# Turning the attention weights of two query tiles in one step of a hybrid attention and convolution encoder layer on Trainium2

## The chip, the cores and the metric

The kernel runs on one core of a Trainium2 chip. The metric is the device time of one execution in microseconds (us), as a median of several runs. The core has five engines that run their own instruction streams and meet at semaphores: PE (TensorE, matrix products and transposes), DVE (VectorE), ACT (ScalarE), POOL (GpSimd) and SP (SyncE, which here only starts transfers).

## What is computed

One encoder layer is applied to a prompt of 2048 frames and to 64 further frames of a running stream, model width 1024. In parallel to a convolution module the layer has an attention of 8 heads of width 64, whose weights come from products of sigmoids and not from a softmax:

```python
def _sb_block(qb, qpos, k, v, kpos):
    z = jnp.einsum('bqhd,bkhd->bhqk', qb, k) * scale
    mask = kpos[None, :] < qpos[:, None]
    log_1m_beta = jnp.where(mask, jax.nn.log_sigmoid(-z), 0.0)
    between = lax.cumsum(log_1m_beta, axis=3, reverse=True) - log_1m_beta
    a = jnp.where(mask, jnp.exp(jax.nn.log_sigmoid(z) + between), 0.0)
    return jnp.einsum('bhqk,bkhd->bqhd', a, v)

def _layer(x, ...):
    proj = _rmsnorm(x, g_mix) @ w_in          # 1024 -> 1024 (conv) + 3 x 512 (q, k, v)
    ...                                        # c: gated causal convolution, LayerNorm, swish, 512x512
    o = _stick_breaking(q, k_all, v_all, q_pos, k_pos)
    x = x + jnp.concatenate([c, o], axis=-1) @ w_out
    f = jax.nn.relu(_rmsnorm(x, g_ff) @ w_ff1) # 1024 -> 4096
    x = x + (f * f) @ w_ff2                    # 4096 -> 1024
```

So a[t, s] = beta[t, s] times the product of (1 - beta[t, j]) over s < j < t, strictly causal, and the output is a @ v.

## The kernel before

**Chunks and windows.** The prompt is worked on in four chunks of 512 frames, 0 to 3. The attention of chunk c + 1 is not a phase of its own: it is spread over the feed-forward of chunk c. `window(c)` walks over 128 slots, 16 for each of 8 parts `e` of the hidden units (18 a part in the last window). A slot is 12 matmuls of 512 columns on PE; slots 0 to 7 of a part are the first product (two slots make one group of hidden units, which ACT takes through relu, square and the high half `hid_hi`, and DVE through the low half `hid_lo`), slots 8 to 15 the second product, whose results DVE adds to `resid`. `att_steps(n, slot)` says which steps of the attention are written behind a slot's own work: two steps a slot for chunk 3 (slots 39 to 115), a little more than one for chunk 2, about one for chunk 1. The attention of chunk 0 and that of the 64 running frames are in the same code.

**Pieces and steps.** A piece is the scores of one head and one query tile of 128 rows (`t` is 0 or 1, the two tiles of a pair) against one block of up to 512 keys. Pieces are numbered through by `z`: chunk 1 has 32 to 95, chunk 2 has 96 to 191, chunk 3 has 192 to 319. The two tiles of a pair follow each other, the even number first. For each head and pair the blocks are walked from the diagonal one (`diag`) back to the first, since the product of (1 - beta) is carried on. Below, step 215 is the step in which the scores of piece 215 are computed. `att_piece(c, step, delay)` gives the piece whose turn it is `delay` steps later. The work on piece z is:

- step z: PE the scores (`scores`, L2498, 2 matmuls) into one of two PSUM banks; DVE the mask of a diagonal piece (L2035); ACT two sigmoids, `stay` = 1 - beta (L1581) and `beta` (L1582), each into one of four buffers.
- step z + 1: DVE the running product over `stay` from the right (the scan, L2047; ahead of it a copy of one column, L2046, for a block that is not diagonal); POOL `beta` times `stay` (L1277).
- step z + 3 (`TURN`): PE turns the weights, one transpose for each 128 keys (`turn`, L2508), into one of two PSUM banks (`T_BANK`, by z % 2); ACT rounds the turned weights to the high half of `aT` (the cast, L1593).
- step z + 4: DVE computes the low half of `aT` as the difference (the low, L2057), which frees the bank.
- step z + 5 (`VALUES`), for the odd tile only: PE multiplies both tiles of the pair by the values (`values`, L2529 in chunks 1 to 3).

When a pair's last block is done, ACT and DVE take the output out of PSUM into `osb` (L2076, L2080) and split it into `ohl` (L2069).

**What waits for what.** The order of instructions on each engine is the order of the code. `turn` waits for POOL's product and for the low of the piece two before, which had the same PSUM bank:

```python
            def turn(q):
                pe.wait_ge(s_a, q.z + 1)
                if q.z >= 2:
                    pe.wait_ge(t_lo, q.z - 1)
```

ACT's sigmoids of piece z wait for `t_ps`, the transposes of piece z - 4, since they write its `beta` buffer. `values` waits for `t_lo` of its odd piece and, at a pair's first block, for `o_sum` (the output of the pair before is out of PSUM). In a slot of the window PE writes the 12 matmuls and then all steps. ACT writes relu and square, the sigmoids of the slot's first step, `hid_hi`, the casts of the first step, and then the second step. DVE writes the scan and low of the first step, the additions to `resid`, the mask, `hid_lo`, and then the scan and low of the second step.

Of the kernel before, what the change touches and what calls it, by code (L numbers as in the profile page):

```python
# [55 lines left out]
TURN, VALUES, TAIL = 3, 5, 9  # L56
# [28 lines left out]
ATT = attention()  # L85


def passes(c):
    return [ATT[c, kind] for kind in range(2 if c == NC - 1 else 1)]
# [6 lines left out]
def att_piece(c, step, delay):  # L96

    for seq in passes(c):
        if step < len(seq) + TAIL:
            k = step - delay  # L100
            return seq[k] if 0 <= k < len(seq) else None
        step -= len(seq) + TAIL
    return None


def att_end(c, what):
# [223 lines left out]
def build(nc, x_prompt, x_sample, cache_k, cache_v, state_conv, g_mix, w_in, w_dw, b_dw, g_cn, b_cn, w_pw,  # L330
# [3 lines left out]
    with ctx:  # L334
# [321 lines left out]
        def stay_of(z):  # L656
            return stay[z % 3] if z < OPENING else stay[z % 4]
# [83 lines left out]
        def out_store(o):  # L741

            return o_st[o % 2], 16 * (o // 2 + 1 + (o == att_end(NC - 1, "o") - 1))
# [5 lines left out]
        def side_by_side(q):  # L749

            return q.o >= att_end(0, "o") and not q.kind

        def summed(o):

            return o + max(0, min(o, att_end(NC - 1, "o") - 1) - att_end(0, "o"))
# [598 lines left out]
        def _(act):  # L1354
# [134 lines left out]
            def front():  # L1489
                evs = kvq_events(1)  # L1490
                for t in range(FRONT):
# [25 lines left out]
                    for step in steps[:1]:  # L1517
                        att_later(0, step)
# [63 lines left out]
                nc.scalar.activation(beta[q.z % 4][0:q.r, 0:q.n], z, ACT.Sigmoid).then_inc(s_sg, 1)  # L1582

            def att_later(c, step):
                q = att_piece(c, step, TURN)
                if q:
                    act.wait_ge(t_ps, q.z + 1)
                    if q.t == 0 and q.v >= 2:
                        act.wait_ge(v_ps, q.v - 1)
                    bank = ps[:, T_BANK + q.z % 2, :]  # L1590
                    full = q.n // P
                    if full:
                        ins = nc.scalar.copy(aT[:, q.v % 2, 0:full, 0, q.t * P:q.t * P + q.r],  # L1593
                                             bank[:, 0:full * q.r].rearrange("p (a b) -> p a b", a=full))
                    if q.n % P:
                        w = q.n % P
                        ins = nc.scalar.copy(aT[0:w, q.v % 2, full, 0, 0:q.r], bank[0:w, full * q.r:(full + 1) * q.r])
                    ins.then_inc(t_hi, 1)
                q = att_piece(c, step, VALUES + 1)
                if q and q.out:  # L1600
                    act.wait_ge(o_sum, summed(q.o + 1))
                    if q.o >= 2:
                        act.wait_ge(*out_store(q.o - 2))
                    me = slice(0, P) if q.kind else slice(q.head % 2 * HD, q.head % 2 * HD + HD)
                    nc.scalar.copy(ohl[q.o % 2][me, 0, :], osb[me, :]).then_inc(o_hi, 1)
                q = att_piece(c, step, VALUES)
                if q and q.out:
                    act.wait_ge(v_ps, q.v + 1)
                    if q.o:
                        act.wait_ge(o_lo, q.o)  # L1610
                    for me, there, here in halves(q):
                        ins = nc.scalar.copy(here(osb[me:me + HD, :]), there(ps[HD - me:P - me, O_BANK, :]))
                    ins.then_inc(o_cp, 1)
# [178 lines left out]
        def _(dve):  # L1792
# [244 lines left out]
            def att_parts(c, step):  # L2037
                q = att_piece(c, step, 1)
                if q:
                    v = stay_of(q.z)  # L2040
                    dve.wait_ge(s_stay, q.z + 1)
                    init = 1.0
                    if not q.diag:
                        dve.wait_ge(s_scan, q.z - 1)
                        init = stay_of(q.z - 2)[0:q.r, 0:1]
                        nc.vector.tensor_copy(v[0:q.r, q.n:q.n + 1], init).then_inc(s_edge, 1)  # L2046
                    nc.vector.tensor_tensor_scan(v[0:q.r, 0:q.n][:, ::-1], v[0:q.r, 0:q.n][:, ::-1],  # L2047
                                                 ones[0:q.r, 0:1].to_broadcast([q.r, q.n]), init,
                                                 ALU.mult, ALU.mult).then_inc(s_scan, 1)
                q = att_piece(c, step, TURN + 1)  # L2050
                if q:
                    dve.wait_ge(t_hi, q.z + 1)
                    bank = ps[:, T_BANK + q.z % 2, :]
                    full = q.n // P
                    o = q.v % 2
                    if full:
                        ins = nc.vector.tensor_tensor(aT[:, o, 0:full, 1, q.t * P:q.t * P + q.r],  # L2057
                                                      bank[:, 0:full * q.r].rearrange("p (a b) -> p a b", a=full),
                                                      aT[:, o, 0:full, 0, q.t * P:q.t * P + q.r].bitcast(F32), ALU.subtract)
                    if q.n % P:  # L2060
                        w = q.n % P
                        ins = nc.vector.tensor_tensor(aT[0:w, o, full, 1, 0:q.r], bank[0:w, full * q.r:(full + 1) * q.r],
                                                      aT[0:w, o, full, 0, 0:q.r].bitcast(F32), ALU.subtract)
                    ins.then_inc(t_lo, 1)
                q = att_piece(c, step, VALUES + 2)
                if q and q.out:
                    me = slice(0, P) if q.kind else slice(q.head % 2 * HD, q.head % 2 * HD + HD)
                    dve.wait_ge(o_hi, q.o + 1)
                    nc.vector.tensor_tensor(ohl[q.o % 2][me, 1, :], osb[me, :], ohl[q.o % 2][me, 0, :].bitcast(F32),  # L2069
                                            ALU.subtract).then_inc(o_lo, 1)  # L2070
                q = att_piece(c, step, VALUES + 1)
                if q and q.out:
                    dve.wait_ge(o_cp, q.o + 1)
                    for me, there, here in halves(q):
                        home = here(osb[me:me + HD, :])
                        ins = nc.vector.tensor_tensor(home, there(ps[me:me + HD, O_BANK, :]), home, ALU.add)  # L2076
                    ins.then_inc(o_sum, 1)
                    if side_by_side(q):
                        dve.wait_ge(o_sum, summed(q.o) + 1)
                        nc.vector.tensor_tensor(home, ps[me:me + HD, O_BANK, 2 * P:4 * P], home, ALU.add).then_inc(o_sum, 1)  # L2080
# [214 lines left out]
        def _(pe):  # L2295
# [244 lines left out]
            def att(c, step):  # L2540
                if q := att_piece(c, step, 0):
                    scores(c, q)
                if q := att_piece(c, step, TURN):
                    turn(q)
                if q := att_piece(c, step, VALUES):
                    values(c, q)
# [229 lines left out]
```

## Time and profile before

| | us |
|---|---|
| median of 3 runs | 2756.15 (2755.06 to 2759.61) |
| the profiled execution, its own time | 2761.99 |
| its span in the trace | 2760.2 |
| PE busy | 2663.6 (96%) |
| DVE busy | 1797.6 (65%) |
| ACT busy | 1121.9 (41%) |
| POOL busy | 592.7 (21%) |

Busy time is the union of an engine's instructions; the span is the time from the first to the last of them. The profiled execution took 5.84 us more than the median and 1.8 us more than its span. Times of day below are us from the start of the span. A row of the timeline gives start, duration, engine, line, operation, operands and how many instructions were merged, and in brackets the idle time of the engine before it and what ended it. The duration of a matmul contains its latency, so what it costs PE is read from one start to the next.

### The profile page before, as it was taken

What the parts mean: (1) busy time and instruction counts of PE and PEld (TensorE: products, weight loads), DVE (VectorE), ACT (ScalarE), POOL (GpSimd) and SP (SyncE); (2) the same over time, 40 slices, a digit from 0 to 9 for tenths busy, and PEclk for the clock granted to TensorE, in tenths of its full rate; (3) what the DMA queues carried; (4) which work ended last, traced back from release to release, by engine and by line L of the source; (5) the groups of instructions that cost most, each with busy time, mean ns of one, the idle gap of its engine ahead of it and who ended that gap; (6) DMA issues with size and microseconds to landing.
All of it is one profiled execution on the core that took longest, in us unless ns stands there. A gap on an engine that the chain in (4) does not pass through costs nothing. (4 is left out here: it accounts for less than half of the span.)

```text
span 2760.2 us, 36720 instructions
## 1 busy us (share of the span) xinstructions
PE 2663.6 (96%) x13304; PEld 2223.3 (81%) x13304; DVE 1797.6 (65%) x2824; ACT 1121.9 (41%) x2221; POOL 592.7 (21%) x523
## 2 busy tenths in 40 slices
PE   8988899999999999999999999999999999999999
PEld 6757778788887887788888797778777877889998
DVE  6996777577773576377775358736888851755444
ACT  4434524455552122355554112334666630333342
POOL 2222210022220010032221002103333310533230
PEclk9999999999999999999999999999999999999999
DMA  9795797697669568455554746854455447355452
GB/s 330 254 351 191 233 354 279 252 332 267 254 219 371 225 228 280 177 218 186 178 181 157 305 183 224 269 197 155 145 191 175 162 161 293 123 189 177 168 198 96
DMA packets 294750, 616.14 MB, mean 223 GB/s; under 512 B 23665, under 2 KB 188529, under 8 KB 250029
## 3 DMA queue, kind: packets, MB, share of 16 engines
q1 hardware_dynamic: 294573, 613.80, 62.8%
q8 instruction: 109, 1.79, 0.3%
q14 instruction: 68, 0.56, 0.1%
HBM read 444.79 MB, written 168.94 MB: 222 GB/s over the span
## 5 line engine op out<-in xcount | busy, mean ns | idle before, releaser
L1277 POOL TENSOR_TENSOR beta<-beta,stay 128x512 f32<-128x512 f32 (+3 forms) x328 | 319.1, 974 | 882.2 <-DVE stay L2047 850.9
L2297 PE MATMUL ps<-h2T_hi,w_s 128*128 128x512 f32 (+2 forms) x976 | 369.6, 379 | 7.6 <-DMA w_s<-w_scratch 3.5
L2299 PE MATMUL ps<-h2T_hi,w_s 128*128 128x512 f32 (+2 forms) x976 | 359.2, 368 | 0.0
L2298 PE MATMUL ps<-h2T_lo,w_s 128*128 128x512 f32 (+2 forms) x976 | 358.7, 367 | 0.0
L1581 ACT ACTIVATE stay<-ps 128x512 f32<-128x512 f32 (+3 forms) x328 | 174.7, 533 | 343.7 <-PE ps L2498 213.3
L2570 PE MATMUL ps<-w_s,hid_hi 128*128 128x512 f32 x768 | 307.2, 400 | 0.0
L2572 PE MATMUL ps<-w_s,hid_hi 128*128 128x512 f32 x768 | 300.1, 391 | 0.0
L2571 PE MATMUL ps<-w_s,hid_lo 128*128 128x512 f32 x768 | 299.6, 390 | 0.0
L2204 DVE TENSOR_TENSOR resid<-ps,resid 128x512 f32<-128x512 f32 x256 | 173.8, 685 | 182.4 <-PE ps L2572 181.9
L2047 DVE TENSOR_TENSOR_SCAN stay<-stay,stay,ones 128x512 f32<-128x512 f32 x192 | 268.7, 1400 | 0.0
L1839 DVE SCALAR_TENSOR_TENSOR cacc<-uT,vecs,cacc 128x512 f32<-128x512 f32 (+1 forms) x360 | 259.7, 777 | 1.5
L2214 DVE TENSOR_TENSOR hid_lo<-ps,hid_hi 128x512 fp32r<-128x512 f32 x96 | 66.2, 690 | 257.3 <-ACT hid_hi L1722 257.3
L2297 PEld LDWEIGHTS ps<-h2T_hi,w_s 128*128 128x128 f32 x976 | 185.1, 190 | 38.7 <-DMA w_s<-w_scratch 3.7
L2299 PEld LDWEIGHTS ps<-h2T_hi,w_s 128*128 128x128 f32 x976 | 184.7, 189 | 30.8
L2298 PEld LDWEIGHTS ps<-h2T_lo,w_s 128*128 128x128 f32 x976 | 185.3, 190 | 27.0 <-issue 1.0
L2057 DVE TENSOR_TENSOR aT<-ps,aT 128x512 fp32r<-128x512 f32 (+3 forms) x328 | 189.5, 578 | 14.1 <-ACT aT L1593 8.2
L2498 PE MATMUL ps<-a_k,a_q 128*128 128x512 f32 (+3 forms) x640 | 185.6, 369 | 9.0 <-DMA a_k<-k_scratch 8.4
L2508 PE MATMUL ps<-ident,beta 128*128 128x128 f32 (+1 forms) x1104 | 175.0, 273 | 10.3 <-DVE aT L2057 10.0
L1593 ACT CAST aT<-ps 128x512 fp32r<-128x512 f32 (+3 forms) x328 | 174.2, 531 | 19.1 <-PE ps L2508 14.6
L1582 ACT ACTIVATE beta<-ps 128x512 f32<-128x512 f32 (+3 forms) x328 | 173.9, 530 | 0.0
L2508 PEld LDWEIGHTS ps<-ident,beta 128*128 128x128 f32 (+1 forms) x1104 | 133.9, 140 | 44.7 <-issue 17.9
L2572 PEld LDWEIGHTS ps<-w_s,hid_hi 128*128 128x128 f32 x768 | 144.2, 188 | 31.8
(268 smaller groups left out, 5640.6 us busy)
## 6 DMA issues: line engine op xcount, KB each, us to landing
w_s<-w_scratch SPq DMA_DIRECT2D x254, 1024.0 KB, 8.0
w_scratch<-w_s SPq DMA_DIRECT2D x94, 1024.0 KB, 8.6
w_raw<-in_w_ff SPq DMA_DIRECT2D x92, 512.0 KB, 5.4
a_k<-k_scratch SPq DMA_DIRECT2D x80, 256.0 KB, 3.7
a_v<-v_scratch SPq DMA_DIRECT2D x80, 256.0 KB, 4.0
a_q<-q_scratch SPq DMA_DIRECT2D x64, 256.0 KB, 4.2
w_s<-w_scratch SPq DMA_DIRECT2D x28, 512.0 KB, 6.5
w_raw<-in_w_in SPq DMA_DIRECT2D x20, 512.0 KB, 8.1
```

The source lines that it names most:

```text
L1277: nc.gpsimd.tensor_tensor(v[0:q.r, 0:n], v[0:q.r, 0:n], stay_of(q.z)[0:q.r, 1:n + 1], ALU.mult).then_inc(s_a, 1)
L1839: nc.vector.scalar_tensor_tensor(out=acc, in0=uT[:, k, tap:tap + wd], scalar=vecs[:, k, tap:tap + 1], in1=acc, op0=ALU.mult, op1=ALU.add). ...
L2047: nc.vector.tensor_tensor_scan(v[0:q.r, 0:q.n][:, ::-1], v[0:q.r, 0:q.n][:, ::-1], ones[0:q.r, 0:1].to_broadcast([q.r, q.n]), init, ALU.mu ...
L2057: ins = nc.vector.tensor_tensor(aT[:, o, 0:full, 1, q.t * P:q.t * P + q.r], bank[:, 0:full * q.r].rearrange("p (a b) -> p a b", a=full), a ...
L2297: nc.tensor.matmul(out, w[0], x[0], start=start, stop=False)
L2298: nc.tensor.matmul(out, w[0], x[1], start=False, stop=False)
L2299: return nc.tensor.matmul(out, w[1], x[0], start=False, stop=stop)
L2498: ins = nc.tensor.matmul(ps[0:q.r, Z_BANK + q.z % 2, 0:q.n], x, a_k[:, k0:k0 + q.n], start=v == 0, stop=v == 1)
L2508: ins = nc.tensor.transpose(ps[0:w, T_BANK + q.z % 2, b * q.r:(b + 1) * q.r], beta[q.z % 4][0:q.r, b * P:b * P + w], ident[0:q.r, 0:q.r])
L2570: nc.tensor.matmul(o, hid_hi[x][:, k, q0:q0 + r], wh[:, c0:c0 + BANK], start=k == 0, stop=False)
L2571: nc.tensor.matmul(o, hid_lo[x][:, k, q0:q0 + r], wh[:, c0:c0 + BANK], start=False, stop=False)
L2572: ins = nc.tensor.matmul(o, hid_hi[x][:, k, q0:q0 + r], wl[:, c0:c0 + BANK], start=False, stop=k == 3)
```

## The change

In chunks 1 to 3, for the prompt's pieces, nothing is turned for the even tile at its own step: its transposes, its cast and its low are written one step later, directly before those of the odd tile. One PE step so has eight transposes in a row (fewer at a diagonal block), four into each of the two banks, and the next step has none; likewise for the two casts on ACT and the two lows on DVE. Steps of scores, sigmoids, scans, products of POOL and `values` stay where they are, and so do chunk 0 and the running frames. No instruction is added or removed and no wait condition is changed.

```diff
@@ -101,6 +101,14 @@
             return seq[k] if 0 <= k < len(seq) else None
         step -= len(seq) + TAIL
     return None
+
+
+def turned_pieces(c, step, delay):
+
+    q = att_piece(c, step, delay)
+    if q is None or (c and not q.kind and q.t == 0):
+        return []
+    return [ATT[c, 0][q.z - ATT[c, 0][0].z - 1], q] if c and not q.kind else [q]
@@ -1582,8 +1590,7 @@
             def att_later(c, step):
-                q = att_piece(c, step, TURN)
-                if q:
+                for q in turned_pieces(c, step, TURN):
                     act.wait_ge(t_ps, q.z + 1)
@@ -2047,8 +2054,7 @@
-                q = att_piece(c, step, TURN + 1)
-                if q:
+                for q in turned_pieces(c, step, TURN + 1):
                     dve.wait_ge(t_hi, q.z + 1)
@@ -2540,7 +2546,7 @@
             def att(c, step):
                 if q := att_piece(c, step, 0):
                     scores(c, q)
-                if q := att_piece(c, step, TURN):
+                for q in turned_pieces(c, step, TURN):
                     turn(q)
                 if q := att_piece(c, step, VALUES):
                     values(c, q)
```

On PE, in the slot of steps 214 and 215 of chunk 3, the order before is this (`beta_147` belongs to piece 211, `beta_144` to piece 212; L2297 begins the next slot):

```order
L2498 MATMUL ps<-a_k,a_q 128x512 [waits s_sg,k_in0]
L2498 MATMUL ps<-a_k,a_q 128x512
L2508 MATMUL ps<-ident,beta_147 128x128 [waits t_lo,s_a]
L2508 MATMUL ps<-ident,beta_147 128x128 x3
L2529 MATMUL ps<-aT,a_v 128x512 [waits o_sum,t_lo,v_in3]
L2529 MATMUL ps<-aT,a_v 128x2x128
L2498 MATMUL ps<-a_k,a_q 128x512 [waits s_sg]
L2498 MATMUL ps<-a_k,a_q 128x512
L2508 MATMUL ps<-ident,beta_144 128x128 [waits t_lo,s_a]
L2508 MATMUL ps<-ident,beta_144 128x128 x3
L2297 MATMUL ps<-h2T_hi_83,w_s 128x512 [waits w_in1]
```

At the same place the changed kernel has this (the lines are 6 higher; `beta_146` belongs to piece 210):

```order
L2504 MATMUL ps<-a_k,a_q 128x512 [waits s_sg,k_in0]
L2504 MATMUL ps<-a_k,a_q 128x512
L2514 MATMUL ps<-ident,beta_146 128x128 [waits t_lo,s_a]
L2514 MATMUL ps<-ident,beta_146 128x128 x3
L2514 MATMUL ps<-ident,beta_147 128x128 [waits t_lo,s_a]
L2514 MATMUL ps<-ident,beta_147 128x128 x3
L2535 MATMUL ps<-aT,a_v 128x512 [waits o_sum,t_lo,v_in3]
L2535 MATMUL ps<-aT,a_v 128x2x128
L2504 MATMUL ps<-a_k,a_q 128x512 [waits s_sg]
L2504 MATMUL ps<-a_k,a_q 128x512
L2303 MATMUL ps<-h2T_hi_83,w_s 128x512 [waits w_in1]
```

The four transposes of the even piece have left the second step; they stand, with their wait for `t_lo`, ahead of those of the odd piece in the first step of the next slot.

On DVE, in steps 213 to 216, the order before is this (`stay_149` is piece 213, `stay_150` 214, `stay_151` 215; L2057 is the low of pieces 210, 211 and 212 in turn):

```order
L2046 COPY stay_149<-stay_151 128x1 [waits s_scan,s_stay]
L2047 SCALAR_TENSOR_TENSOR stay_149<-stay_149,stay_151,ones 128x512
L2057 TENSOR_TENSOR aT<-ps,aT 128x4x128 [waits t_hi]
L2069 TENSOR_TENSOR ohl_154<-osb,ohl_154 64x256 [waits o_hi]
L2046 COPY stay_150<-stay_148 128x1 [waits s_scan,s_stay]
L2047 SCALAR_TENSOR_TENSOR stay_150<-stay_150,stay_148,ones 128x512
L2057 TENSOR_TENSOR aT<-ps,aT 128x4x128 [waits t_hi]
L2046 COPY stay_151<-stay_149 128x1 [waits s_scan,s_stay]
L2047 SCALAR_TENSOR_TENSOR stay_151<-stay_151,stay_149,ones 128x512
L2057 TENSOR_TENSOR aT<-ps,aT 128x4x128 [waits t_hi]
L2035 TENSOR_TENSOR ps<-ps,limit 128x128 [waits z_ps]
L2214 TENSOR_TENSOR hid_lo_103<-ps,hid_hi_102 128x512 [waits f_hi]
```

In the changed kernel it is this (L2063 is now the low, of pieces 210 and 211 together):

```order
L2053 COPY stay_149<-stay_151 128x1 [waits s_scan,s_stay]
L2054 SCALAR_TENSOR_TENSOR stay_149<-stay_149,stay_151,ones 128x512
L2075 TENSOR_TENSOR ohl_154<-osb,ohl_154 64x256 [waits o_hi]
L2053 COPY stay_150<-stay_148 128x1 [waits s_scan,s_stay]
L2054 SCALAR_TENSOR_TENSOR stay_150<-stay_150,stay_148,ones 128x512
L2063 TENSOR_TENSOR aT<-ps,aT 128x4x128 [waits t_hi] x2
L2053 COPY stay_151<-stay_149 128x1 [waits s_scan,s_stay]
L2054 SCALAR_TENSOR_TENSOR stay_151<-stay_151,stay_149,ones 128x512
L2042 TENSOR_TENSOR ps<-ps,limit 128x128 [waits z_ps]
L2220 TENSOR_TENSOR hid_lo_103<-ps,hid_hi_102 128x512 [waits f_hi]
```

A scan is now followed by no low or by two: the low of piece 210 has moved behind the scan of 214, and that of 212 behind the mask and `hid_lo`.

## Rows read from the trace of the kernel before

**Rows 1.** The page, its first line and part 1: engine, busy us, share, instructions.

```profile
span 2760.2 us, 36720 instructions
PE 2663.6 (96%) x13304; PEld 2223.3 (81%) x13304; DVE 1797.6 (65%) x2824; ACT 1121.9 (41%) x2221; POOL 592.7 (21%) x523
```

**Rows 2.** Windows, chunks 1 to 3: PE, PEld, DVE, ACT, POOL busy; PEclk, DMA share, GB/s.

```profile
559.00:816.00 257.00, 254.12 (x1236) 210.36 (x1235) 201.98 (x316) 152.96 (x303) 58.64 (x63) 1.00 0.77 274
1164.00:1486.00 322.00, 320.16 (x1575) 264.77 (x1576) 232.93 (x384) 170.70 (x367) 94.56 (x95) 0.99 0.53 185
1884.00:2226.00 342.00, 333.93 (x1700) 273.52 (x1698) 293.02 (x473) 216.56 (x457) 134.80 (x128) 1.00 0.49 163
```

**Rows 3.** Waits of PE, 1884 to 2226: total us, times, longest us.

```profile
PE ps L2508 <- DVE aT L2057: 7.5, 12, 0.8
```

**Rows 4.** Source line L2508, 559 to 816: idle before it until (us, times).

```profile
  DVE aT L2057: 0.4, 1
```

**Rows 5.** Source line L2508, 1164 to 1486: idle before it until (us, times).

```profile
  DVE aT L2057: 0.2, 1
```

**Rows 6.** Timeline of PE, 1997.5 to 1999.3, four transposes between matmuls.

```profile
1998.09 0.60 PE L2508 MATMUL ps<-ident,beta 128*128 128x128 f32 x4
1998.44 0.48 PE L2570 MATMUL ps<-w_s,hid_hi 128*128 128x512 f32 x1
1998.76 0.39 PE L2571 MATMUL ps<-w_s,hid_lo 128*128 128x512 f32 x1
1998.99 0.40 PE L2572 MATMUL ps<-w_s,hid_hi 128*128 128x512 f32 x1
```

**Rows 7.** Timeline of PE, 880 to 882, eight transposes of another tensor.

```profile
880.59 1.10 PE L2320 MATMUL ps<-ident,xin 128*128 128x128 f32 x8 [1.45 <-DVE xin L1815]
881.44 0.47 PE L2715 MATMUL ps<-w_s,mixT_hi 128*128 128x512 f32 x1
881.75 0.39 PE L2716 MATMUL ps<-w_s,mixT_lo 128*128 128x512 f32 x1
```

**Rows 8.** Timeline of PE, 1935 to 1962: transposes of pieces 211, 212, 215, 216 and 220.

```profile
1935.96 0.60 PE L2508 MATMUL ps<-ident,beta 128*128 128x128 f32 x4
...
1936.75 0.62 PE L2498 MATMUL ps<-a_k,a_q 128*128 128x512 f32 x2
1938.13 0.63 PE L2508 MATMUL ps<-ident,beta 128*128 128x128 f32 x4 [0.77 <-DVE aT L2057]
...
1947.22 0.60 PE L2508 MATMUL ps<-ident,beta 128*128 128x128 f32 x4
...
1949.74 0.52 PE L2508 MATMUL ps<-ident,beta 128*128 128x128 f32 x3 [0.52 <-DVE aT L2057]
...
1961.44 0.63 PE L2508 MATMUL ps<-ident,beta 128*128 128x128 f32 x4 [0.58 <-DVE aT L2057]
```

**Rows 9.** Timeline of DVE, 1937 to 1947, with steps 213 to 217.

```profile
1937.33 0.66 DVE L2057 TENSOR_TENSOR aT<-ps,aT 128x512 fp32r<-128x512 f32 x1
1937.91 1.01 DVE L2069 TENSOR_TENSOR ohl<-osb,ohl 64x256 fp32r<-64x256 f32 x1
...
1938.91 1.26 DVE L2047 TENSOR_TENSOR_SCAN stay<-stay,stay,ones 128x512 f32<-128x512 f32 x1
...
1940.74 1.74 DVE L2047 TENSOR_TENSOR_SCAN stay<-stay,stay,ones 128x512 f32<-128x512 f32 x1
...
1942.99 0.28 DVE L2035 TENSOR_TENSOR ps<-ps,limit 128x128 f32<-128x128 f32 x1
1944.73 0.69 DVE L2214 TENSOR_TENSOR hid_lo<-ps,hid_hi 128x512 fp32r<-128x512 f32 x1 [1.47 <-ACT hid_hi L1722]
1945.34 0.95 DVE L2047 TENSOR_TENSOR_SCAN stay<-stay,ones 128x384 f32<-128x384 f32 x1
```

**Rows 10.** Timeline of POOL, 1940 to 1942, the product of piece 214.

```profile
1940.31 1.10 POOL L1277 TENSOR_TENSOR beta<-beta,stay 128x512 f32<-128x512 f32 x1 [1.67 <-DVE stay L2047]
```

## The prediction

> **What bounds the kernel now.** I read the page first: PE is busy for 2663.6 of 2760.2 us, every other engine far less [rows 1], so only what PE waits for, or what it takes longer over, can move the time. Then I cut out the three stretches that the change touches. PE is busy for 254.12 of 257 us in chunk 1, 320.16 of 322 in chunk 2 and 333.93 of 342 in chunk 3 [rows 2]: some 3, 2 and 8 us of idle are all that can be won there by removing waits. The waits of PE say whose they are. In chunk 3 nearly all of it is one line: the transposes L2508 wait 12 times, 7.5 us in all, for the low L2057 of DVE [rows 3]; in chunk 1 that wait is 0.4 us once and in chunk 2 0.2 us once [rows 4, 5]. DVE is the engine to watch in chunk 3, busy for 293.02 of 342 us, 86% [rows 2]: late at places, not the bound on average.
>
> **How one such wait arises.** The reader is to see it in step 215. The scores of 215 start at 1936.75, two matmuls of 0.23 us each, so the transposes of piece 212 could start at 1937.21. They start at 1938.13, 0.92 us late (0.77 of it counted as idle) [rows 8]. They need the PSUM bank of piece 210, whose low starts at 1937.33 and takes 0.66, to 1937.99 [rows 9], and 0.14 later PE goes. It is the even tile's transposes that wait, for a low that DVE has behind a scan of the same slot. The waits come three to a part of 16 slots, in four parts, at slots of the first product in which `hid_lo` has come late: 12 waits at about 0.77 + 0.52 + 0.58 of idle by part (pieces 212, 216, 220) [rows 8]; with the 0.15 that a start loses beyond the counted idle (0.92 against 0.77) they cost 7.5 + 12 x 0.15 = 9.3 us. Chunks 1 and 2 add 0.4 + 0.2 + 2 x 0.15 = 0.9. That makes 10.2 us that the change can touch.
>
> **The parts of the change.**
>
> Transposes in one row. A group of four costs PE from 1998.09 to 1998.76, less the one matmul in between (0.23, from 1998.76 to 1998.99): 0.44 us, so 0.11 for each, with hardly anything for the change between matmul and transposes [rows 6]. Two groups cost 0.88. For eight in a row the nearest row is that of another tensor: 880.59 to 881.75 less 0.23 is 0.93, with a start out of an idle PE in it [rows 7]. So a merged pair costs between nothing (and perhaps the few ns of the one transition less, at most 0.01) and 0.05 more, over 144 pairs between -1 and +7 us. The 0.05 belongs to the start from idle, which hardly one of these groups has, so I take 0.
>
> The removed wait. With the change the transposes of the even piece leave the step in which they wait, and come after the 12 matmuls and the scores of the next slot, 12 x 0.23 + 0.46 = 3.2 us later. All 12 waits of chunk 3, and those of chunks 1 and 2, vanish at their place: -10.2 us.
>
> The wait that takes its place. Both pieces' lows are now in one step, and the eight transposes need the two lows of the pair before. I walk DVE through the stretch of rows 9. Today it runs low 210, `ohl`, scan 214, low 211, scan 215, low 212 and the mask without a gap. With the change it runs low 208 and 209 before, then `ohl`, scan 214, low 210, low 211, scan 215 and the mask: the same number of lows, since the one more ahead is made up by low 212, which goes behind the mask. One thing is saved: scan 215 lasts 1.74, not 1.26, because it starts while POOL's product of 214 still has 0.67 to run (1940.74 against an end at 1941.41) [rows 9, 10]; behind two lows of 0.58 (1937.33 to 1937.91) it starts after POOL is through. So the mask comes about 0.4 earlier, at 1942.6, and by the chain mask, sigmoids, `hid_hi`, `hid_lo` the latter at 1944.3 in place of 1944.73 [rows 9]. From there: `hid_lo` 0.6, scan of 216 0.9, low 212 to 1946.4, low 213 to 1947.0. PE, 0.92 ahead, wants to start the transposes of 214 at 1947.22 - 0.92 = 1946.3 [rows 8]; it must wait for low 212 and the 0.15 behind it, to 1946.55: 0.25. Those of 215 would follow 0.44 later, at 1947.0, and wait for low 213, to 1947.15: 0.15. Of 0.92 us 0.4 has come back. The second wait of the part (0.52 + 0.15) comes after that and has no follower, as DVE has then only scans and lows: I allow 0.15. The third (0.58 + 0.15) leads to a diagonal piece like the first, but with a narrow one, 0.35. Sum by part: 2.3 removed, 0.9 new, 1.4 to 1.5 net; four parts, 6 us. Chunks 1 and 2: 0.9 removed, and I let half of it come back, 0.4 net. No term here reaches beyond the attention: behind chunk 3 PE goes on with work that is not held by a transfer, and a gain of PE shifts the rest.
>
> Later sigmoids. ACT's sigmoids of an even piece z need the transposes of z - 4, which now stand behind the scores of z in the same step: up to 0.44 us later. Then two casts of some 0.6 in a row stand before the sigmoids of z + 1. Behind them wait `hid_hi`, `hid_lo` and the scans. In a slot with hidden units relu and square stand ahead and hide the 0.44. Elsewhere DVE's scan of z comes after the addition to `resid`, and is delayed by part of it; the scores that need the sigmoid's bank come two steps, so a slot of 12 x 0.23 = 2.8 us and more, later. Cost taken: 0; if the cover were gone it would be 0.44 in each of 64 pairs of chunk 3, up to 28 us, the bound above. DMA issues: the change moves none on any queue, and the waits of SP are on scores and values, which keep their steps.
>
> A port between DVE and POOL. Scan 215 ends at 1942.48, 1.07 after POOL's product; `ohl` is stretched to 1.01 in the same way [rows 9, 10]. In a slot without other DVE work two scans now stand back to back, and the second may be held for the whole 1.10 of the product instead of 0.47. In turn the scan behind two lows is free. Per slot: before twice 0.47, after once up to 1.1: nothing by rows, +0.15 at worst, and DVE has 49 us of idle over chunk 3. The Trainium skill (SBUF — State Buffer, "SBUF: two separate sides") states that a DVE instruction with two SBUF inputs and a GpSimd instruction lock the shared port pair for a whole instruction and the other one blocks. By that rule the held second scan is certain where both are ready, and the rule speaks against putting two scans together. The trace agrees that a scan is held until the product ends; the sum stays, as the rule gives the freed scan back too.
>
> Sum: 0 - 10.2 + 4 x 0.9 + 0.5 = **-6.1 us**. The profiled execution would go from 2761.99 to 2756, the median of runs, which is 5.84 below it, from 2756.15 to 2750.
>
> **The rivals.** (a) The forecast: most of the waits in chunk 3 vanish, two fifths return; 2750, with an own range of 2745 to 2753. (b) The wait only moves: DVE is the bound of those stretches, its work is the same, and PE waits at the eight transposes for as long as it did at four. For it speaks that DVE runs without a gap from low 210 to the mask [rows 9]; against it that 1.47 us of idle follow the mask. Time: 2756, 2753 to 2758. (c) Slower: the second of two lows is late everywhere in chunk 3. It ends 0.58 later than a single one and is needed only 0.44 later, so where DVE is the bound each odd piece's transposes wait 0.14, and 0.15 for the start. For 64 pairs that is 64 x 0.29 = 18.6, less the 9.3 removed there: +9, 2765. It decides from the point at which DVE has no idle left in a slot, busy near 97%; it is at 86% and would be held further by the adjacent scans and ACT's later sigmoids, which act in this direction. (d) The clock: the Trainium skill (TensorE: Matmul & The Clock Gate, "PE-mode transpose") states that transposes do not count as busy time for the clock gate, so that a longer row of them could lower the clock. Here the granted clock is 1.00, 0.99 and 1.00 of full in the three stretches with groups of four [rows 2], and eight in a row ran at 0.11 each [rows 7]; that the clock falls to 1.2 GHz for 5% of chunk 3 would cost 342 x 0.05 / 2 = 9 us, less the gain of 6 that is +3, 2759. I hold it for unlikely: the row of transposes is 0.9 us between 5 us of matmuls.
>
> **How the numbers follow.** Chances: (a) 0.60, (b) 0.28, (c) 0.09, (d) 0.03. The range takes in the most that can be won (10.2 + 1 below 2756.15, 2745) with 2 us for the spread of the medians (runs lie 2755.06 to 2759.61), and reaches up over (b) to the near half of (c): 2743 to 2760. No change is what lies within 0.2%, 5.5 us, which is about what a measurement of this kernel can tell; so the forecast of -6.1 is only just outside of it. From (a) 0.48 is faster (its middle and lower half) and 0.12 the same, (b) is the same, from (c) and (d) 0.07 is slower and 0.05 the same: faster 0.48, same 0.45, slower 0.07.
>
> **What would show it.** In the profile after, the wait of the transposes for the low falls in chunk 3 from 12 times and 7.5 us to under 3 us, now in front of the diagonal slots and in pieces 0.1 to 0.3 long; PE's idle of chunk 3 from 8 to about 3. A scan of 1.7 us follows directly on a scan, none follows on two lows. Eight transposes cost 0.88 from start to start. It is wrong if the eight transposes wait as long as before (b), if `values` or L2297 gets waits for DVE that it has not (c), if the matmuls' pitch in these stretches is no longer 0.23 (d), or if ACT's later sigmoids leave DVE idle before its scans by so much that the lows are late for the next slot.

## The result

The changed kernel takes 2742.38 us in the median of 4 runs (2737.83 to 2744.26) against 2755.61 for the kernel before (2755.01 to 2759.61): 13.2 us saved. The measured ratio of the two is 0.9943 with a 95% interval of 0.9932 to 0.9955; it is not that of the medians (0.9952), and by it 15.7 us are saved (12.4 to 18.7). I had forecast 2750, 6.1 us saved, and a range of 2743 to 2760. The direction is right, the size is off by a factor of two and more, and the time is below the range.

Page of the changed kernel, first line and part 1, as in [rows 1]:

```profile
span 2739.8 us, 36720 instructions
PE 2650.6 (97%) x13304; PEld 2225.4 (81%) x13304; DVE 1768.8 (65%) x2824; ACT 1123.3 (41%) x2221; POOL 619.4 (23%) x523
```

The spans of the two profiled executions differ by 20.4 us, more than the medians: the one of before was itself 6.4 above the median of its four runs, the one after 0.8 below its own. Where that lies is seen at chunk 1's first scores, ahead of which nothing is changed. They start at 558.3 before and at 552.9 after. So the chunks have to be compared by their own length, from the first scores to the last. In the source view of the scores line the two times behind the durations are these. Before, chunks 1, 2 and 3:

```profile
L2498 PE MATMUL ps<-a_k,a_q x128: 220/389/398, 558.3 to 810.7; 128*128 128x512 f32 x80, 128*128 128x128 f32 x16, 128*128 128x256 f32 x16, 128*128 128x384 f32 x16
L2498 PE MATMUL ps<-a_k,a_q x192: 220/389/485, 1161.3 to 1484.0; 128*128 128x512 f32 x144, 128*128 128x128 f32 x16, 128*128 128x256 f32 x16, 128*128 128x384 f32 x16
L2498 PE MATMUL ps<-a_k,a_q x256: 220/390/504, 1881.3 to 2220.2; 128*128 128x512 f32 x104, 128*128 128x128 f32 x8, 128*128 128x256 f32 x8, 128*128 128x384 f32 x8
```

After:

```profile
L2504 PE MATMUL ps<-a_k,a_q x128: 220/389/393, 552.9 to 804.6; 128*128 128x512 f32 x80, 128*128 128x128 f32 x16, 128*128 128x256 f32 x16, 128*128 128x384 f32 x16
L2504 PE MATMUL ps<-a_k,a_q x192: 220/389/398, 1155.5 to 1474.0; 128*128 128x512 f32 x144, 128*128 128x128 f32 x16, 128*128 128x256 f32 x16, 128*128 128x384 f32 x16
L2504 PE MATMUL ps<-a_k,a_q x256: 220/389/504, 1870.2 to 2200.3; 128*128 128x512 f32 x104, 128*128 128x128 f32 x8, 128*128 128x256 f32 x8, 128*128 128x384 f32 x8
```

Chunk 1 goes from 252.4 to 251.7 us, chunk 2 from 322.7 to 318.5, chunk 3 from 338.9 to 330.1: 0.7 + 4.2 + 8.8 = 13.7 us, close to the difference of the medians. Some 1.2 of chunk 2's 4.2 is chance: at its start 7 matmuls run at half clock, where 15 did before. A second profile of the changed kernel (`e11_changed_again` below) has 251.6, 320.4 and 330.0 us. So one profile gives chunk 3 to 0.1 us, but chunk 2 only to some 2 us.

The waits of PE in chunk 3, as in [rows 3]:

```profile
PE ps L2514 <- DVE aT L2063: 0.7, 3, 0.4
PE ps L2504 <- ACT beta L1590: 0.5, 1, 0.5
```

The wait that bounded my gain is gone, from 7.5 us to 0.7. And PE is nearly full in chunk 3, 340.01 of 342 us against 333.93, while DVE's busy time falls from 293.02 [rows 2] to 283.58 (a window of the same length in the changed kernel):

```profile
1870.00:2212.00 342.00, 340.01 (x1746) 284.74 (x1745) 283.58 (x478) 220.75 (x465) 144.98 (x128) 1.00 0.51 171
```

What the waits don't show is in PE's timeline. The same kind of slot, 12 matmuls, follows a row of four transposes before; its first matmul starts at 1998.44 [rows 6] and the scores behind it at 2001.28, 2.84 us. After, the slot follows two scores, and then comes the row of eight:

```profile
1984.04 0.62 PE L2504 MATMUL ps<-a_k,a_q 128*128 128x512 f32 x2
1984.49 0.39 PE L2576 MATMUL ps<-w_s,hid_hi 128*128 128x512 f32 x1
...
1987.21 0.62 PE L2504 MATMUL ps<-a_k,a_q 128*128 128x512 f32 x2
1987.67 1.03 PE L2514 MATMUL ps<-ident,beta 128*128 128x128 f32 x8
1988.46 1.05 PE L2535 MATMUL ps<-aT,a_v 128*128 128x512 f32 x4
```

The slot takes 1984.49 to 1987.21, 2.72 us: 0.12 less. Of it 0.09 is the first matmul (0.32 to the next one in [rows 6], 0.23 here), which my price of 0.44 had in it; the other 0.03 is spread over the ten behind it. Taken from the starts of all such matmuls of chunk 3, the first ones left out, the mean step falls from 230.1 to 227.6 ns (229.1 to 227.8 in chunk 1, 229.5 to 227.4 in chunk 2). PE is counted as busy in both, so no view of waits or shares shows it.

### The profile page after: what moved, and what is told of

Same layout as the page of the kernel before. It is cut to its first block and busy times, and to the rows that moved or that the text cites. A ratio compares the mean times of both kernels' runs of the same rounds, so it can differ in the third digit from the quotient of the medians.

```text
span 2739.8 us, 36720 instructions
## 1 busy us (share of the span) xinstructions
PE 2650.6 (97%) x13304; PEld 2225.4 (81%) x13304; DVE 1768.8 (65%) x2824; ACT 1123.3 (41%) x2221; POOL 619.4 (23%) x523
## 5 line engine op out<-in xcount | busy, mean ns | idle before, releaser
L1285 POOL TENSOR_TENSOR beta<-beta,stay 128x512 f32<-128x512 f32 (+3 forms) x328 | 353.6, 1081 | 831.8 <-DVE stay L2054 794.3
L2303 PE MATMUL ps<-h2T_hi,w_s 128*128 128x512 f32 (+2 forms) x976 | 362.5, 371 | 7.2 <-DMA w_s<-w_scratch 3.2
L2305 PE MATMUL ps<-h2T_hi,w_s 128*128 128x512 f32 (+2 forms) x976 | 357.7, 367 | 0.0
L2576 PE MATMUL ps<-w_s,hid_hi 128*128 128x512 f32 x768 | 300.7, 392 | 0.0
L2578 PE MATMUL ps<-w_s,hid_hi 128*128 128x512 f32 x768 | 299.2, 390 | 0.0
L2054 DVE TENSOR_TENSOR_SCAN stay<-stay,stay,ones 128x512 f32<-128x512 f32 x192 | 257.4, 1342 | 0.0
L2063 DVE TENSOR_TENSOR aT<-ps,aT 128x512 fp32r<-128x512 f32 (+3 forms) x328 | 180.0, 585 | 12.7 <-ACT aT L1600 7.2
L2578 PEld LDWEIGHTS ps<-w_s,hid_hi 128*128 128x128 f32 x768 | 144.2, 188 | 30.6
L2576 PEld LDWEIGHTS ps<-w_s,hid_hi 128*128 128x128 f32 x768 | 144.2, 188 | 30.6 <-DVE hid_lo L2220 0.2
L2577 PEld LDWEIGHTS ps<-w_s,hid_lo 128*128 128x128 f32 x768 | 144.2, 188 | 29.8 <-issue 0.5
L1600 ACT CAST aT<-ps 128x512 fp32r<-128x512 f32 (+3 forms) x328 | 157.4, 538 | 18.8 <-PE ps L2514 14.3
```

Of the source, the lines that this page charges most:

```text
L1285: nc.gpsimd.tensor_tensor(v[0:q.r, 0:n], v[0:q.r, 0:n], stay_of(q.z)[0:q.r, 1:n + 1], ALU.mult).then_inc(s_a, 1)
L2303: nc.tensor.matmul(out, w[0], x[0], start=start, stop=False)
L2305: return nc.tensor.matmul(out, w[1], x[0], start=False, stop=stop)
L2576: nc.tensor.matmul(o, hid_hi[x][:, k, q0:q0 + r], wh[:, c0:c0 + BANK], start=k == 0, stop=False)
L2577: nc.tensor.matmul(o, hid_lo[x][:, k, q0:q0 + r], wh[:, c0:c0 + BANK], start=False, stop=False)
L2578: ins = nc.tensor.matmul(o, hid_hi[x][:, k, q0:q0 + r], wl[:, c0:c0 + BANK], start=False, stop=k == 3)
```

## The experiments

Two reasons were to be told apart, for the time beyond my forecast above all. The wait theory: all that was won are waits for DVE. The row theory: a row of transposes has a price besides its transposes, and 144 rows fewer are worth some 0.05 us each. Times below are medians, with the ratio to the kernel before, measured beside it, and its interval; what is saved is taken from the ratio. "Length" is that of chunk 3 as above: 338.9 before, 330.1 in the changed kernel. "Pitch" is the step from one feed-forward matmul to the next, a slot's first one left out.

**Parts of the change.** `e1_chunks_1_2` and `e2_chunk_3` pair the pieces in some chunks only:

```diff
-    if q is None or (c and not q.kind and q.t == 0):
+    both = c in (1, 2)      # e2: (3,)
+    if q is None or (both and not q.kind and q.t == 0):
         return []
-    return [ATT[c, 0][q.z - ATT[c, 0][0].z - 1], q] if c and not q.kind else [q]
+    return [ATT[c, 0][q.z - ATT[c, 0][0].z - 1], q] if both and not q.kind else [q]
```

> The change in chunks 1 and 2 alone (80 of the 144 pairs); chunk 3 as before. Row theory: a row of transposes costs PE, beside 0.11 us for each, a fixed part at its end (the next matmuls run late for up to a slot), so that every merged pair saves about 0.05 us wherever it is: 2.4 + 1.4 us in these chunks, with their few waits 3.5 to 4.5 us below the kernel before. Wait theory: all that is won are waits for DVE's lows, of which these chunks had 0.9 us: 0 to 1 us below before.

> The change in chunk 3 alone (64 pairs). Row theory: 9.4 us removed waits less about 3 that come back, and 64 x 0.05 = 3 us for the merged rows, together 8.5 to 10 us below before; the two partial kernels add up to the full change. Wait theory: 6 us below before.

Measured: e1 2754.33, ratio 0.9981 (0.9972 to 0.9990), so 5.2 us saved where there was hardly a wait (0.6 us [rows 4, 5]). e2 2746.27, ratio 0.9954 (0.9942 to 0.9967), 12.7 us saved; chunk 3 has length 330.1, as in the changed kernel, and 338.9 in e1. The wait theory falls with e1. e2's 12.7 is more than the 8.8 of its chunk 3, and the lower end of its interval (9.1) is just above it; what the rest is, the trace doesn't show.

**Late, but not merged.** `e3_four_and_four` keeps the late step and puts the scores between the two rows of four:

```diff
             def att(c, step):
+                turned = turned_pieces(c, step, TURN)
+                for q in turned[:-1]:
+                    turn(q)
                 if q := att_piece(c, step, 0):
                     scores(c, q)
-                for q in turned_pieces(c, step, TURN):
+                for q in turned[-1:]:
                     turn(q)
```

> As the changed kernel, even piece one step later on all engines, but the four transposes of the even piece stand ahead of the step's scores and those of the odd piece behind them: two rows of four again, with the late step kept. Row theory: the saving of the merged rows is lost, 5 to 7 us slower than the changed kernel, still some 6 below before. Wait theory: the time of the changed kernel within 1 us, or up to 2 slower because the first four need their bank 0.46 us earlier.

Measured: 2746.84, ratio 0.9956 (0.9943 to 0.9968), 12.1 us saved; length 331.9. That is in between the two expectations. In the trace the pitch of the feed-forward matmuls stays low (227.5 to 227.6 ns) although the rows are split, so the place of a row counts and not only the number.

**More rows.** `e4_two_and_two` splits the transposes of the kernel before (`turn(t, 0)` issues the first half of them, `turn(t, 1)` the second):

```diff
             def att(c, step):
+                t = att_piece(c, step, TURN)
+                split = t is not None and c in (1, 2)
+                if split:
+                    turn(t, 0)
                 if q := att_piece(c, step, 0):
                     scores(c, q)
-                if q := att_piece(c, step, TURN):
-                    turn(q)
+                if t:
+                    turn(t, 1 if split else None)
```

> The kernel before, with the four transposes of each piece of chunks 1 and 2 split in two rows of two, one ahead of the step's scores and one behind them (nothing later, no pairs): 160 rows more. Row theory: 160 x 0.05 = 8 us slower than before, and the split shows in the pitch of the matmuls. Wait theory, or a price for transposes only and none for rows: within 1 us of before.

Measured: 2763.55, ratio 1.0009 (0.9999 to 1.0019). The 8 us did not come. Chunks 1 and 2 are 0.4 and 1.6 us longer (252.8 and 324.3), with 1.8 us more of waits for lows that are now needed earlier and 1.0 less at half clock. PE's idle time and the half clock apart, 0.5 and 1.3 us are left for the 128 rows that the trace has more (a piece of one block can't be split, and some halves have no scores between them): 0.014 us a row. A row that is followed, two matmuls later, by another costs little.

**Where the row stands.** `e5_transposes_last` is the changed kernel with `values` ahead of `turn`; `e6_transposes_first` is the kernel before with `turn` ahead of `scores`:

```diff
 # e5
                 if q := att_piece(c, step, 0):
                     scores(c, q)
-                for q in turned_pieces(c, step, TURN):
-                    turn(q)
                 if q := att_piece(c, step, VALUES):
                     values(c, q)
+                for q in turned_pieces(c, step, TURN):
+                    turn(q)
 # e6
+                if q := att_piece(c, step, TURN):
+                    turn(q)
                 if q := att_piece(c, step, 0):
                     scores(c, q)
-                if q := att_piece(c, step, TURN):
-                    turn(q)
```

> The changed kernel with the eight transposes behind the step's products with the values, not ahead of them. In chunks 1 and 2, where most slots have one step, they then stand directly ahead of a slot's 12 feed-forward matmuls, as the rows of four did in the kernel before; in chunk 3 they stand ahead of two score matmuls. Place theory (the matmuls of a slot run at 229 to 230 ns and not 227 for some ten matmuls if transposes stand directly ahead of them, which was 5 us over the three chunks): the pitch goes back up in chunks 1 and 2, 1.5 to 3 us slower there, and stays at 227 in chunk 3. In chunk 3 the lows have 0.9 us more, so the 1.5 us of waits for them go: together within 2 us of the changed kernel. Row theory (only the number of rows counts): the pitch stays as in the changed kernel everywhere.

> The kernel before, with each piece's four transposes ahead of the step's scores and not behind them; no pairs, nothing later. Place theory: no row of transposes stands directly ahead of a slot's matmuls any more, so their pitch falls from 229.5 to 227.5 ns as in the changed kernel, 4 to 5 us over the three chunks, without any merging. Against it the bank is needed 0.46 us earlier: the 13 waits for DVE's lows in chunk 3 grow by 0.46 each and new ones come, 6 to 9 us. Together 1 to 5 us slower than before; in chunks 1 and 2 alone 1 to 3 us faster. If the pitch comes from the pairs or the late lows it stays at 229.5.

Measured: e5 2770.27, ratio 1.0044 (1.0031 to 1.0056), 12 us slower than before, with a length of 344.8. I had looked only at the lows. The longest waits of its chunk 3 name what I had left out:

```profile
PE ps L2535 <- DVE osb L2086: 11.2, 8, 1.7
```

`values` at a pair's first block waits for the output sums L2086 of the pair before; in the changed kernel the eight transposes ahead of it cover most of that wait. What I could read of the pitch is that slots directly behind a row take 2.82 to 2.86 us in chunks 1 and 2 again, as the place theory has it. e6: 2767.12, ratio 1.0030 (1.0018 to 1.0041), 8 us slower, waits for the lows 10.9 us. But its slots, two scores behind a row, still take 2.75 to 2.76 us, and the pitch falls about half way, to 228.5 to 228.8 ns. So "directly ahead of" was too narrow: two scores are not enough to get past the effect of a row. In the changed kernel most slots of chunk 3 have six matmuls between the row and themselves (2.73 us), and some four in ten of chunks 1 and 2 have no row among the 13 matmuls ahead of them (2.72 to 2.73).

Place and number can be told apart in chunks 1 and 2. Here are their lengths less PE's idle time and what matmuls at half clock took longer; between two traces of the same code they differ by up to 0.2 us:

| | chunk 1 | chunk 2 |
|---|---|---|
| before: rows of four, directly ahead of slots | 249.2 | 315.6 |
| e3: rows of four, one step later | 248.1 | 314.0 |
| e5: rows of eight, directly ahead of slots | 248.7 | 314.0 |
| the changed kernel: rows of eight, not directly ahead | 248.0 | 313.3 |

The changed kernel saves 3.5 us, 0.044 for each of the 80 pairs. Three quarters of it come without any merging (e3, 2.7 us) and over half with merging at the old place (e5, 2.1 us), so place and number each win a part alone, and the parts overlap.

**The length of the row.** `e12_each_transpose_twice` issues every transpose of chunks 1 and 2 of the kernel before twice:

```diff
-            def turn(q):
+            def turn(q, times=1):
...
                 for b, w in unit_blocks(q):
-                    ins = nc.tensor.transpose(...)
+                    for _ in range(times):
+                        ins = nc.tensor.transpose(...)
...
-                    turn(q)
+                    turn(q, 2 if c in (1, 2) else 1)
```

> The kernel before, every transpose of chunks 1 and 2 issued twice (528 more, the same result twice): as many rows as before, of twice the length, nothing paired or later. Tail theory (a row costs 0.109 us for each transpose and, whatever its length, a tail in the matmuls behind it): 528 x 0.109 = 57.6 us longer, and the row's tail as before: the first matmul behind it at 316 ns, the slot of 12 matmuls behind it at 2.84 to 2.85 us, the pitch at 229.5. Length theory (the tail grows with the row): the slots behind the rows get longer, over 2.9 us, and the total is 60 us or more; then merging rows could not have saved it.

Measured: 2811.05, ratio 1.0200 (1.0183 to 1.0217), 55 us for 544 further transposes (I had counted 528). The slot behind a row of eight takes 2.82 to 2.83 us (2.85 behind four before) and its first matmul 315 to 316 ns (316 to 318): twice the length, no longer tail. In the traces of chunks 1 and 2, waits and clock apart, a further transpose costs 0.10 us. This is what I had needed: a longer row costs its transposes only, and what it costs behind them is paid once.

**Where DVE's lateness comes from.** In the timeline each of the waits of chunk 3 comes behind a slot in which `hid_lo` is late, since ACT writes `hid_hi` only after two sigmoids that themselves wait for DVE's mask. `e7_high_half_first` moves it ahead of them in the changed kernel, `e10_high_half_first_no_pairs` in the kernel before:

```diff
+                    if group is not None:
+                        act.wait_ge(f_sq, f + 1)
+                        nc.scalar.copy(hid_hi[x][:, j, s0:s0 + w], bank).then_inc(f_hi, 1)
                     for step in steps[:1]:
                         att_sigmoids(n, step)
-                    if group is not None:
-                        act.wait_ge(f_sq, f + 1)
-                        nc.scalar.copy(hid_hi[x][:, j, s0:s0 + w], bank).then_inc(f_hi, 1)
```

> The changed kernel, and on ACT in each slot that ends a group of hidden units the high half hid_hi ahead of the sigmoids of the slot's first step. The waits left in chunk 3 (1.5 us for lows, 1.5 us for the output sums, 0.5 in the pitch between transposes) come behind a late hid_lo on DVE: if that chain (mask, sigmoids, hid_hi, hid_lo, scan, lows) is their cause, hid_lo comes 1 us earlier, they vanish and 2 to 3.5 us are won. If DVE's work alone is the cause: no change within 1 us.

> The kernel before with hid_hi ahead of the sigmoids on ACT, nothing paired. If the 12 waits of chunk 3 come from a late hid_lo (the chain mask, sigmoids, hid_hi, hid_lo), they vanish with this alone: 7 to 9 us below before, with the pitch of the feed-forward matmuls still at 229.5 ns; then the changed kernel's waits and its rows are two separate gains. If the waits come from where the even piece's transposes stand, most of them stay: within 3 us of before.

Measured: e10 2748.33, ratio 0.9958 (0.9946 to 0.9970), 11.6 us saved; length 329.4, 9.5 less, with the pitch as before (229.8 ns against 230.1). e7 2739.13, ratio 0.9930 (0.9918 to 0.9943); length 326.7. All waits of PE on DVE in chunk 3 are gone in e7, and all but one in e10 (waits of PE, e7 and then e10):

```profile
PE ps L2504 <- ACT beta L1590: 0.3, 1, 0.3
```

```profile
PE ps L2498 <- ACT beta L1582: 0.3, 1, 0.3
PE ps L2508 <- DVE aT L2057: 0.3, 1, 0.3
```

These two differ by the pairs alone, and neither has waits: 329.4 - 326.7 = 2.7 us for 64 pairs, 0.042 us a pair. That is the clean price of pairing, place and number of rows together. The four traces with chunk 3 of the kernel before lie at 338.8 to 339.0, the three with that of the changed kernel at 330.0 to 330.1, so it stands well clear of the spread. Chunks 1 and 2 agree: less idle time and half clock, e7 is 1.2 us shorter in chunk 1 (32 pairs) and 2.4 in chunk 2 (48 pairs) than e10. Of the 2.7 us, 1.3 are in the steps of the feed-forward matmuls behind a slot's first, 0.9 in those of the scores and `values`, and 0.4 in the rows with the matmul behind them.

**Sums before lows.** `e8_sums_before_lows` is the changed kernel with DVE's output low and output sums ahead of the two lows (the whole loop over the turned pieces moves):

```diff
             def att_parts(c, step):
...
-                for q in turned_pieces(c, step, TURN + 1):
-                    dve.wait_ge(t_hi, q.z + 1)
...
                 q = att_piece(c, step, VALUES + 2)
...
                 q = att_piece(c, step, VALUES + 1)
...
+                for q in turned_pieces(c, step, TURN + 1):
+                    dve.wait_ge(t_hi, q.z + 1)
...
```

> The changed kernel with DVE's output sums and low half of the output ahead of the two lows of the step. The four waits of the products with the values for the sums (1.5 us) vanish. The lows come 0.8 us later at those four steps, and the transposes there had 0.2 to 0.4 us to spare: four new waits of about 0.5 us each. Sum: no change within 1 us; slower by 2 or more if the lows are what DVE is late with everywhere.

Measured: 2752.25, ratio 0.9980 (0.9971 to 0.9989), some 8 to 10 us slower than the changed kernel by its two ratios (0.9950 of e11, 0.9943), 2.8 of it in chunk 3 (length 332.9). The waits for the sums went and those for the lows grew to 3.9 us in 8, twice what I had forecast. The same reordering is in chunk 0, whose scores take 86.3 us against 83.6, and in chunk 2 (321.5 against 318.5, or 320.4 in e11); I had not thought of it.

**Again, and further.** `e11_changed_again` is the changed kernel; `e9_high_half_first_all_chunks` is e7 with the pairs in chunk 0 too (the condition on `c` dropped from `turned_pieces`).

> The changed kernel once more, beside the two others of this call: some 13 us below before by every theory.

> The changed kernel with hid_hi first and the pairs in chunk 0 as well (16 pairs more). By the rows' price of 0.045 us a pair 0.7 us below the version with hid_hi first alone, so 3 to 5 us below the changed kernel; slower than that if chunk 0, whose stay buffers are only three, stalls on the later casts.

Measured: e11 2745.79, ratio 0.9950 (0.9937 to 0.9964), in agreement with 0.9943. e9 2742.26, ratio 0.9933 (0.9919 to 0.9948): no gain over e7's 0.9930 that could be told. e7, the changed kernel with `hid_hi` first, has the lowest ratio. In chunk 3 it is 3.4 us shorter than the changed kernel, though the intervals of the whole times overlap.

## Why the prediction was right or wrong

**The step that failed: "Transposes in one row ... so I take 0".** I priced a row of four at 0.44 us, from its first transpose to the second matmul behind it [rows 6], and eight at twice that, against 0.93 of another row [rows 7]. Both numbers leave out the slower step of the next ten matmuls, which only a comparison of whole slots shows (2.84 against 2.72), and doubling 0.44 hid a small part that is paid once per row. I also asked only what a row costs and not what stands behind it, though e3 shows that this is the larger part. My bound was -1 to +7 us. Measured it is 0.042 us a pair (e10 against e7), 6 us over 144 pairs, and e12 shows that the part behind a row does not grow with it. Nearly all of what my forecast lacked is this term: -6.1 - 6 = -12.1, against -13.2 by the medians, -13.7 by the lengths of the chunks and -15.7 (-12.4 to -18.7) by the ratio.

**The removed wait: right.** The transposes' waits in chunk 3 fell from 7.5 us [rows 3] to 0.7. Their full price was 9.3 in my sum; e10, which removes waits and leaves the rows, shortens chunk 3 by 9.5.

**The wait that takes its place: right in size, wrong in its places.** I forecast 3.6 us to come back in chunk 3; e7 against the changed kernel says 330.1 - 326.7 = 3.4. But I had put 0.4 of each part at pieces 214 and 215, and there is none. DVE after, from `hid_lo` to the scan of 215, as in [rows 9]:

```profile
1921.58 0.69 DVE L2220 TENSOR_TENSOR hid_lo<-ps,hid_hi 128x512 fp32r<-128x512 f32 x1 [2.78 <-ACT hid_hi L1729]
...
1925.99 0.39 DVE L2075 TENSOR_TENSOR ohl<-osb,ohl 64x256 fp32r<-64x256 f32 x1
...
1926.37 1.27 DVE L2054 TENSOR_TENSOR_SCAN stay<-stay,stay,ones 128x512 f32<-128x512 f32 x1
1927.56 1.26 DVE L2063 TENSOR_TENSOR aT<-ps,aT 128x512 fp32r<-128x512 f32 x2
...
1928.80 1.27 DVE L2054 TENSOR_TENSOR_SCAN stay<-stay,stay,ones 128x512 f32<-128x512 f32 x1
```

`ohl` takes 0.39 and not 1.01, the scan of 215 1.27 and not 1.74: both holds by POOL of [rows 9, 10] are gone, where I had freed only the scan. What did come back stands at pieces 220 and 221, before a narrow diagonal piece. In PE's timeline after, the scores there are two matmuls of 128 columns only, so that the row could follow them near 1950.6:

```profile
1950.43 0.33 PE L2504 MATMUL ps<-a_k,a_q 128*128 128x128 f32 x2
1950.90 1.23 PE L2514 MATMUL ps<-ident,beta 128*128 128x128 f32 x8
1951.89 1.16 PE L2535 MATMUL ps<-aT,a_v 128*128 128x512 f32 x4
```

The row starts some 0.3 late and takes 0.99, where it takes 0.85 at the same place of e7, which has no waits there: the wait of the third kind, that I had put at 0.35, measured 0.44. The rest is a wait that I did not have, four times about 0.4 in `values` for the output sums, which stand behind two lows (1.13 us) and no longer behind one. I named `values` only among the signs of (c). So 0.8 us a part are found, 3.3 in four parts.

**Chunks 1 and 2: wrong, by the same term.** I forecast 0.4 us; the partial kernel e1 saved 5.2 (2.8 to 7.7). Merging accounts for 80 x 0.042 = 3.4 of it.

**Later sigmoids: right.** DVE's scans wait for the sigmoids 13.7 us in 24 times, before and after alike, and nothing of it reaches PE.

**A port between DVE and POOL: not quite harmless, and in both directions.** I expected the second of two adjacent scans to be held. In the pair of scans above POOL was held instead (POOL's timeline of the changed kernel; three products, which take 1.1 us each when nothing holds them):

```profile
1926.20 5.81 POOL L1285 TENSOR_TENSOR beta<-beta,stay 128x512 f32<-128x512 f32 x3 [1.45 <-DVE stay L2054]
```

Over chunk 3, of the 96 scans of 128x512 that carry a start in, 34 are longer than 1.4 us before and 21 after (16.3 and 9.7 us above 1.27 each); of the 13 that follow directly on a scan (a copy of one column between them) 4 are. What I had put at "+0.15 at worst" is more in one place of each part. DVE ahead of the row of 1950.90:

```profile
1948.11 1.93 DVE L2054 TENSOR_TENSOR_SCAN stay<-stay,stay,ones 128x512 f32<-128x512 f32 x1
1950.07 1.29 DVE L2063 TENSOR_TENSOR aT<-ps,aT 128x512 fp32r<-128x512 f32 x2
```

The scan begins while POOL's product of 1947.68 to 1948.96 runs and takes 0.66 longer than 1.27. The first low follows on it at once, though its cast was done at 1948.20, and PE's row starts 0.14 after that low. So the held scan is what this wait of 0.44 comes from, as far as the trace can say; no run takes the hold away alone.

**The rivals.** (b), the wait only moves: no. (c), slower through the second low: no in the sum, but e8 ran into it at the lows, and e5 into the like of it at the output sums, when the little room there was used up. (d), the clock: no, 1.00 in chunk 3 with rows of eight. The chance of 0.48 for faster was too low because the sum lacked a term, not because of the rivals.

**What stays open.** Why matmuls behind a row run up to 7 ns slow for about ten steps, and how the price depends on what stands behind the row. The merged pairs say 0.042 us, the split rows of e4 0.014 a row, where another row follows two matmuls later. I have no experiment that gives one rule for both.

## What to carry to other kernels

Where PE is the bound, a group of short instructions is to be priced with and without it, over the whole stretch up to where the steps are regular again, and not by its own rows: what it costs behind its end is counted as busy time and depends on what stands there. Here both fewer and longer groups and a place away from long regular stretches won a part. A stall that comes at fixed places is followed back through the engines' written orders to the first late link. Here moving one instruction on ACT took 9.5 us of waits out of chunk 3, where moving the transposes took 6.1 net (8.8 less the 2.7 of the pairs), and both together gave the shortest chunk 3. And before work is moved away from ahead of a wait, ask what it covers there.

## What the hardware showed unexpectedly

Matmuls of 512 columns have a step of 227 ns when nothing disturbs them and 227 to 234, on the mean 230, for about ten steps behind a row of transposes (316 for the first). A further 128x128 transpose in a row costs 0.10 to 0.11 us. DVE's scan and POOL's product hold each other up in both directions: a scan of 1.27 us lasts 1.74 or 1.93 when the product has started [rows 9, 10], and three products of 1.1 us take 5.81 together while `ohl` and two scans run beside them at their usual 0.39 and 1.27.
